# The last layer norm of a two-layer encoder: token tile by token tile, with its scaling done on TensorE

## Chip, cores and metric

One core of one Trainium2 chip runs the whole kernel in one launch. The metric is the device time of that launch in microseconds. Before the change it is 2288.3 us, the median of 3 executions (2286.69 to 2289.38).

## What is computed

A trunk of two layers works on 256 tokens of 2048 features in float32. Each layer is a mixer and a gated MLP, and each of the four sub-layers ends in a residual sum and a layer norm. Cut to what matters here:

```python
def layer_norm(x, g, b):
    mu = jnp.mean(x, axis=-1, keepdims=True)
    var = jnp.mean(jnp.square(x - mu), axis=-1, keepdims=True)
    return (x - mu) * lax.rsqrt(var + LN_EPS) * g + b

for l in range(2):
    ...
    u = x * (1.0 + sc2) + sh2
    y = conv_ffn(u, w_up[l], conv_w[l], conv_b[l], w_down[l])
    x = layer_norm(ALPHA * x + (1.0 + g2) * y, ln_g[l, 1], ln_b[l, 1])
return x
```

The change touches only the last of the four norms, the one whose result is the output.

## The kernel before

The kernel is one hand-ordered program for each engine; semaphores are waited on in the order written. Weights come in units of 2048 columns through four raw slots; ScalarE makes the high part of each (`hi_unit`, L598), VectorE the low part (L939), and TensorE multiplies (L1440 and L1572, L1580) in the one-record format that the profile calls fp32r. The 256 tokens are two token tiles of 128 rows, t = 0 and 1; the 2048 features are four chunks of 512 columns, c or n = 0 to 3. `x` holds both tiles in SBUF.

The end of the program is the phase `(1, "down_b")`: for each chunk c, six units of products into a pair of banks, one bank for each token tile. VectorE's `tail(c)` inside `y_out` (L1040) then multiplies the pair with the gate, adds it to `x`, takes the statistics (`bn_stats`) and, for chunks 0 to 2 of this phase, multiplies `x` with the norm's weight at once (L1076). The very last unit is computed by token tile (`by_tile`, L1444 to L1458): tile 0 is complete (`y_half`) about 2 us before tile 1 (`w_used`), so that VectorE starts on tile 0 (L1045 to L1048) while TensorE works on tile 1 (then L1050 to L1056).

After it comes the last norm, which is in three places:

- TensorE, at the end of its program (L1944 to L1955). It first puts the norm's bias, a product of the identity with `lnp[:, 1]`, into six banks (chunks 0 to 2, two tiles; L1948). Then it waits for `tail_diag` and adds to each of the six banks the product of a diagonal matrix, which holds minus mean times root for every token, with the norm's weight `lnp[:, 0]` (L1953). Both operands of these products are plain f32. "Root" is the reciprocal root of the variance, `rs`.
- VectorE, `layer_norm(3, True)` (L1091 to L1122): the aggregate of the statistics, the variance, the root by ScalarE's Sqrt (L762), a reciprocal and one correction step (L1085 to L1089), the two diagonals (L1104), the whole affine step of chunk 3 in four instructions (L1108, L1112), and then for chunks 0 to 2 one instruction for each bank: `x` times root plus bank (L1119, six instructions).
- SyncE (L577 to L581): four output transfers, one for each chunk with both tiles, 512 KB each, in the order 3, 0, 1, 2, each behind its own count of `ln_affine`.

ScalarE has only the Sqrt in this stretch. Banks: `TAIL_BANKS` gives chunks 0, 1, 2 the banks 0, 4, 6 (plus t); the last chunk's sums are in banks 2 and 3, which the norm doesn't use before.

Of the kernel before, what the change touches and what calls it, by code (L numbers as in the profile page):

```python
# [13 lines left out]
D = 2048  # L14
S = 256
P = 128
F = 5504
KT = D // P
NT = S // P
NCOL = 512  # L20
# [15 lines left out]
EPS = 1e-5  # L36
# [46 lines left out]
OUT_ORDER = [(c, j) for c in (0, 1, 2) for j in (0, 1)] + [(c, j) for c in (0, 1, 2) for j in (2, 3)]  # L83
OUT_ORDER += [(3, j) for j in range(4)]
OUT_BANKS = (0, 2, 4, 0)
TAIL_ORDER = (3, 0, 1, 2)
TAIL_BANKS = {0: 0, 1: 4, 2: 6}
Y_LAST = {((0, "out"), 3): 1, ((0, "down_b"), 3): 2, ((1, "o"), 3): 3, ((1, "down_b"), 3): 4}
OUT_LAST = {IN_UNITS + OUT_ORDER.index((c, 3)): c for c in range(4)}
LR_SLOT, GATE_SLOT = 17, 19  # L90
# [117 lines left out]
def build(nc, A, out):  # L208
# [4 lines left out]
    PH = plan()  # L213

    ctx = ExitStack()
    with ctx:
# [8 lines left out]
        def place(name, shape, at, dt=f32):  # L225
            return nc.alloc_sbuf_tensor_at(name, shape, dt, offset=at)
# [60 lines left out]
        w_lrh = place("w_lr_hi", [P, KT, GRANK], r_s + 10240, f32r)  # L287
        w_lrl = place("w_lr_lo", [P, KT, GRANK], r_s + 10240 + 1024, f32r)
        acc_alt = place("ada_acc_alt", [P, 2 * NCOL], r_s + 4096)
        tail_diag = place("tail_diag", [P, NT, P], r_s)  # L290
        att_hi = place("att_hi", [P, NT, 3 * D], r_w, f32r)

        qkT = place("qk_T", [P, 2, 2 * S], r_s)
# [137 lines left out]
        def _(sp):  # L431
# [142 lines left out]
                    ln_load(2)  # L574
            mlp(1, 16)
            out_v = out[0].rearrange("(t p) n -> p t n", p=P)
            for i, n in enumerate(TAIL_ORDER):  # L577
                sp.wait_ge(sem("ln_affine"), 13 + i)
                sp.dma_start(out_v[:, :, n * NCOL:(n + 1) * NCOL], x[:, :, n * NCOL:(n + 1) * NCOL]
                             ).then_inc(sem("out_done"), 16)  # L580
            sp.wait_ge(sem("out_done"), 4 * 16)  # L581


        @block.scalar
        def _(act):
# [333 lines left out]
                    ins.then_inc(sem("att_p"), 1)  # L919
            ln_sd(2)  # L920
            mlp(1)
            ln_sd(3)


        @block.vector
        def _(dve):
# [109 lines left out]
            def y_out(key, first, stats, banks=(0, 2, 0, 2), ends=None):  # L1036
# [3 lines left out]
                def tail(c):  # L1040
                    y = Y0[key] + c
                    cs = slice(c * NCOL, (c + 1) * NCOL)
                    if (key, c) in Y_LAST:
# [12 lines left out]
                        nc.vector.bn_stats(bn[:, 1, c, :], x[:, 1, cs]).then_inc(y_done, 1)  # L1056
                        return
# [33 lines left out]
            def layer_norm(s, last, after=None):  # L1091
                dve.wait_ge(y_done, {0: 4, 1: 12, 2: 16, 3: 24}[s])
# [4 lines left out]
                if not last:  # L1097
                    ln_quarters(s, 0, 4 if s == 1 else 2)
                dve.wait_ge(sem("ln_var"), s + 1)
                rstd(var, sd, rs, t1, "ln_var", "ln_sd", s + 1)  # L1100
                if last:
                    link(nc.vector.scalar_tensor_tensor(t1, mv[:, :, 0], -1.0, rs, ALU.mult, ALU.mult))
                    for t in range(NT):
                        ins = nc.vector.tensor_scalar(tail_diag[:, t, :], ident, t1[:, t:t + 1], None, ALU.mult)  # L1104
                    ins.then_inc(sem("tail_diag"), 1)
                    cs = slice(3 * NCOL, D)
                    for t in range(NT):
                        ins = nc.vector.scalar_tensor_tensor(x[:, t, cs], x[:, t, cs], mv[:, t, 0:1],  # L1108
                                                             lnp[:, 0, cs], ALU.subtract, ALU.mult)
                    link(ins)  # L1110
                    for t in range(NT):
                        ins = nc.vector.scalar_tensor_tensor(x[:, t, cs], x[:, t, cs], rs[:, t:t + 1],  # L1112
                                                             lnp[:, 1, cs], ALU.mult, ALU.add)
                    ins.then_inc(sem("ln_affine"), 1)
                    for n in range(3):
                        cs = slice(n * NCOL, (n + 1) * NCOL)
                        dve.wait_ge(sem("tail_shift"), n + 1)
                        for t in range(NT):
                            ins = nc.vector.scalar_tensor_tensor(x[:, t, cs], x[:, t, cs], rs[:, t:t + 1],  # L1119
                                                                 bank[TAIL_BANKS[n] + t][:, :], ALU.mult, ALU.add)  # L1120
                        ins.then_inc(sem("ln_affine"), 1)
                    return  # L1122
# [7 lines left out]
                u_lo(U_LN[s], slice(0, 2), 0)  # L1130
                u_lo(U_LN[s] + 1, slice(2, 4), 1)
                lo_unit(after)

            def ln_lo(s, v):
                u_lo(U_LN[s] + v, slice(2 * v, 2 * v + 2), v % 2)
# [149 lines left out]
            for s in range(FRONT_UNITS):  # L1285
# [72 lines left out]
            layer_norm(0, False, unit_no((0, "up_a"), 0, 1))  # L1358
            mlp(0)
            layer_norm(1, False, ATT_U + 1)  # L1360
            o_tail = y_out((1, "o"), True, True, ends={c: ATT_U + s for c, s in O_LAST.items()})
            for u in range(ATT_UNITS):
                if u in SLOT_S:
# [34 lines left out]
                if u < 4:  # L1398
                    ln_affine(1, u)
                beside(ATT_U + u)  # L1400
            layer_norm(2, False, unit_no((1, "up_a"), 0, 1))
            mlp(1)
            layer_norm(3, True)


        @block.gpsimd
# [15 lines left out]
        def _(pe):  # L1422
# [520 lines left out]
            mlp(1)  # L1943
            pe.wait_ge(acc_free, evacuated((1, "down_b"), 2) + 1)  # L1944
            pe.wait_ge(sem("ln_in"), 32 * 4)
            for n in range(3):
                for t in range(NT):
                    nc.tensor.matmul(bank[TAIL_BANKS[n] + t][:, :], ident, lnp[:, 1, n * NCOL:(n + 1) * NCOL],  # L1948
                                     start=True, stop=False)
            pe.wait_ge(sem("tail_diag"), 1)  # L1950
            for n in range(3):
                for t in range(NT):
                    ins = nc.tensor.matmul(bank[TAIL_BANKS[n] + t][:, :], tail_diag[:, t, :],  # L1953
                                           lnp[:, 0, n * NCOL:(n + 1) * NCOL], start=False, stop=True)
                ins.then_inc(sem("tail_shift"), 1)  # L1955


_INS = ["x", "c", "w_ada", "b_ada", "ln_g", "ln_b", "w_in_ab", "w_gate_lr", "b_gate", "gla_norm_g", "w_pool",
# [39 lines left out]
```

## Time and profile before

| | us |
|---|---|
| median of 3 executions | 2288.3 |
| the profiled execution, its own time | 2294.48 |
| span of its trace, first to last instruction | 2292.6 |

| engine | busy us | share of the span |
|---|---|---|
| TensorE, matmuls (PE) | 2241.7 | 98% |
| TensorE, weight loads (PEld) | 1859.4 | 81% |
| VectorE (DVE) | 1695.1 | 74% |
| ScalarE (ACT) | 1009.2 | 44% |
| GpSimd (POOL) | 8.4 | 0% |

The DMA engines move 612.66 MB at a mean of 267 GB/s. The mean granted TensorE clock is 0.990 of full speed. Times in the trace count from the span's start. Matmuls are pipelined and their ends are modelled, so the starts of successive records give the pace, and the sum of their durations doesn't. A plain f32 product of 512 columns shows as two records.

### The profile page before, as it was taken

Reading aid. Unit: us, or ns where it says so; the run is one execution under the profiler, and the core shown is the slowest. Engines: PE = TensorE matmul, PEld = TensorE weight load, DVE = VectorE, ACT = ScalarE, POOL = GpSimd, SP = SyncE. Lnnn points to the kernel's source line nnn. Section 1 sums busy time; section 2 is a strip of 40 time slices with the busy share of each in tenths; the row PEclk is TensorE's granted clock in tenths of the full one; section 3 lists DMA queues with packets and bytes.
Section 4 is the critical chain, followed back from the end, with each engine's and each line's share of the span. In section 5 each row is a group of like instructions: output and inputs, shape, how many; then the busy total and the mean of one; then the engine's idle time right before and its main releaser. Section 6 shows DMA issues by size and latency. Waiting matters only on the chain. (4 is left out here: it accounts for less than half of the span.)

```text
span 2292.6 us, 27917 instructions
## 1 busy us (share of the span) xinstructions
PE 2241.7 (98%) x11205; PEld 1859.4 (81%) x11205; DVE 1695.1 (74%) x1671; ACT 1009.2 (44%) x1011; POOL 8.4 (0%) x19
## 2 busy tenths in 40 slices
PE   7999998999999999999999999999999999999999
PEld 3777776788888888888788888878888888888886
DVE  2889899768888777888877767685688755665665
ACT  2445343454433444443355444435544334445432
POOL 1000000000000000000000000000000000000000
PEclk9999999999999999999999999999999999999999
DMA  9999889867879988789877777865678766566653
GB/s 373 381 409 346 296 298 342 290 201 257 297 269 336 317 274 286 267 281 328 325 262 275 272 262 258 285 240 159 208 259 298 252 200 201 185 192 193 219 191 105
DMA packets 392227, 612.66 MB, mean 267 GB/s; under 512 B 21113, under 2 KB 205073, under 8 KB 390562
## 3 DMA queue, kind: packets, MB, share of 16 engines
q1 hardware_dynamic: 387314, 608.29, 76.0%
q10 hardware_dynamic: 4336, 2.33, 0.3%
q8 instruction: 89, 1.46, 0.2%
q14 instruction: 40, 0.33, 0.0%
q0 software_dynamic: 448, 0.25, 0.0%
HBM read 608.70 MB, written 2.10 MB: 266 GB/s over the span
## 5 line engine op out<-in xcount | busy, mean ns | idle before, releaser
L939 DVE TENSOR_TENSOR w_lo<-w_raw,w_hi 128x2048 fp32r<-128x2048 f32 x380 | 847.8, 2233 | 392.5 <-ACT w_hi L598 342.1
L598 ACT ACTIVATE w_hi<-w_raw 128x2048 fp32r<-128x2048 f32 x380 | 710.1, 1870 | 836.4 <-PE banks L1440 508.2
L1572 PE MATMUL banks<-u_hl,w_hi 128*128 128x512 f32 x2368 | 575.6, 392 | 3.3 <-ACT hid_tok L638 1.8
L1572 PEld LDWEIGHTS banks<-u_hl,w_hi 128*128 128x128 f32 x2368 | 432.9, 188 | 90.3 <-ACT hid_tok L638 2.7
L1440 PE MATMUL banks<-w_hi,u_hl 128*128 128x512 f32 x1920 | 482.1, 404 | 11.4 <-ACT u_hl L663 3.6
L1440 PEld LDWEIGHTS banks<-w_hi,u_hl 128*128 128x128 f32 x1920 | 364.7, 193 | 97.1 <-issue 16.1
L1580 PEld LDWEIGHTS banks<-u_hl,w_lo 128*128 128x128 f32 x2368 | 308.4, 191 | 15.5 <-DVE w_lo L939 1.2
L1580 PE MATMUL banks<-u_hl,w_lo 128*128 128x256 f32 x2368 | 313.3, 283 | 0.3 <-DVE w_lo L939 0.3
L1440 PE MATMUL banks<-w_hi,hid_hi 128*128 128x512 f32 x688 | 270.1, 393 | 0.0
L1440 PE MATMUL banks<-w_hi,hid_lo 128*128 128x512 f32 x688 | 267.8, 389 | 0.0
L955 DVE SCALAR_TENSOR_TENSOR ada_acc<-ada_w,silu_c,ada_acc 128x1024 f32<-128x1024 f32 x187 | 239.3, 1280 | 20.1 <-DMA ada_w<-in_w_ada 14.3
L1440 PE MATMUL banks<-w_lo,u_hl 128*128 128x512 f32 x960 | 238.0, 390 | 2.8 <-DVE w_lo L939 2.8
L1440 PEld LDWEIGHTS banks<-w_lo,u_hl 128*128 128x128 f32 x960 | 180.0, 188 | 41.9 <-DVE w_lo L939 4.5
L1440 PE MATMUL banks<-w_lo,hid_hi 128*128 128x512 f32 x688 | 172.3, 390 | 1.5 <-DVE w_lo L939 1.5
L1440 PEld LDWEIGHTS banks<-w_lo,hid_hi 128*128 128x128 f32 x688 | 128.9, 188 | 29.5 <-DVE w_lo L939 2.8
L1440 PEld LDWEIGHTS banks<-w_hi,hid_hi 128*128 128x128 f32 x688 | 129.2, 188 | 28.7 <-ACT w_hi L598 1.3
L1440 PEld LDWEIGHTS banks<-w_hi,hid_lo 128*128 128x128 f32 x688 | 129.2, 188 | 27.4 <-issue 1.0
L955 DVE SCALAR_TENSOR_TENSOR ada_acc_aux<-ada_w,silu_c,ada_acc_aux 128x1024 f32<-128x1024 f32 x75 | 96.0, 1280 | 7.9 <-DMA ada_w<-in_w_ada 6.2
L837 ACT ACTIVATE conv<-conv 128x512 f32<-128x512 f32 (+1 forms) x44 | 27.4, 623 | 134.6 <-DVE conv L1191 134.6
L955 DVE SCALAR_TENSOR_TENSOR ada_acc_alt<-ada_w,silu_c,ada_acc_alt 128x1024 f32<-128x1024 f32 x48 | 61.6, 1283 | 6.5 <-DMA ada_w<-in_w_ada 3.1
L1191 DVE SCALAR_TENSOR_TENSOR conv<-g_sum,cols,conv 128x255 f32<-128x255 f32 (+1 forms) x148 | 65.0, 479 | 1.4
L623 ACT ACTIVATE g_sum<-banks 128x512 f32<-128x512 f32 (+1 forms) x38 | 22.2, 585 | 95.5 <-PE banks L1580 95.5
(229 smaller groups left out, 1252.1 us busy)
## 6 DMA issues: line engine op xcount, KB each, us to landing
ada_w<-in_w_ada SPq DMA_DIRECT2D x352, 512.0 KB, 6.7
w_raw<-in_w_up SPq DMA_DIRECT2D x344, 512.0 KB, 4.7
w_raw<-in_w_down SPq DMA_DIRECT2D x152, 512.0 KB, 4.9
w_raw<-in_w_qkv SPq DMA_DIRECT2D x96, 512.0 KB, 4.7
w_raw<-in_w_in_ab SPq DMA_DIRECT2D x64, 512.0 KB, 8.9
ada_w_more<-in_w_ada SPq DMA_DIRECT2D x32, 512.0 KB, 11.0
w_raw<-in_w_out_ab SPq DMA_DIRECT2D x32, 512.0 KB, 6.1
w_raw<-in_w_o SPq DMA_DIRECT2D x32, 512.0 KB, 4.9
```

The source lines that it names most:

```text
L598: nc.scalar.activation(whi[:, u % HL_SLOTS, 0:width], raw[:, u % RAW_SLOTS, 0:width], ACT.Copy).then_inc(w_hi, 1)
L623: nc.scalar.activation(g_sum[:, 0:nf, :], pair[b // 2][:, 0:nf, S:2 * S], ACT.Copy).then_inc(g_low, 1)
L837: nc.scalar.activation(gc[:, 0:nf, :], gc[:, 0:nf, :], ACT.Gelu_apprx_tanh).then_inc(h_gelu, 1)
L939: nc.vector.tensor_tensor(wlo[:, u % HL_SLOTS, 0:width], raw[:, u % RAW_SLOTS, 0:width], whi[:, u % HL_SLOTS, 0:width].bitcast(f32), ALU.s ...
L955: nc.vector.scalar_tensor_tensor(acc[:, :], w, silu_c[:, r:r + 1], acc[:, :], ALU.mult, ALU.add).then_inc(a_step, 1)
L1191: ins = nc.vector.scalar_tensor_tensor(gc[:, k, lag:S], src, cols[:, at:at + 1], gc[:, k, lag:S], ALU.mult, ALU.add)
L1440: return nc.tensor.matmul(banks[t][:, 0:width], u_at(kt, t), w[:, slot, k * width:(k + 1) * width], start=start, stop=stop)
L1572: ins = nc.tensor.matmul(bank[banks[s] + i][:, :], tile(whi, k, s, i), uhl[:, kt].rearrange("p a s -> p (a s)"), start=first and k == 0, s ...
L1580: ins = nc.tensor.matmul(bank[banks[s] + i][:, S:2 * S], tile(wlo, k, s, i), uhi[:, kt, :], start=False, stop=last and k == len(kts) - 1)
```

## The change

The last norm is done by token tile. All eight outputs (four chunks, two tiles) now get a bank with bias and mean term on TensorE, chunk 3 in banks 2 and 3. For five of them, all four of tile 0 and chunk 1 of tile 1 (`TAIL_ACT`), TensorE also adds the third term: a second diagonal, of the root itself, times `x` (which has been multiplied with the weight before). The bank then holds the finished output, and ScalarE copies it to `x`. The other three (`TAIL_DVE`: chunks 0, 3 and 2 of tile 1) are finished by VectorE as before. Statistics, root and diagonals are made for each tile by itself, on columns of one element. Each output has its own transfer of 256 KB, eight in all, in the order in which TensorE gets to them. The chain of the correction step is one instruction shorter (r·r·v in one). The early return in `tail` moves the end of chunk 3 into the new function `last_norm`.

```diff
+TAIL_BANKS = {0: 0, 1: 4, 2: 6, 3: 2}
+TAIL_ACT = [(0, 0), (0, 1), (0, 2), (0, 3), (1, 1)]
+TAIL_DVE = [(1, 0), (1, 3), (1, 2)]
...
-        tail_diag = place("tail_diag", [P, NT, P], r_s)
+        tail_diag = place("tail_diag", [P, NT, 2, P], r_s)
...
-            for i, n in enumerate(TAIL_ORDER):
-                sp.wait_ge(sem("ln_affine"), 13 + i)
-                sp.dma_start(out_v[:, :, n * NCOL:(n + 1) * NCOL], x[:, :, n * NCOL:(n + 1) * NCOL]
-                             ).then_inc(sem("out_done"), 16)
-            sp.wait_ge(sem("out_done"), 4 * 16)
+            sent = 0
+            for by, done in ((TAIL_ACT[:4], "tail_act"), (TAIL_DVE[:1], "tail_dve"), (TAIL_ACT[4:], "tail_act"),
+                             (TAIL_DVE[1:], "tail_dve")):
+                for t, n in by:
+                    order = TAIL_ACT if done == "tail_act" else TAIL_DVE
+                    sp.wait_ge(sem(done), order.index((t, n)) + 1)
+                    sp.dma_start(out_v[:, t, n * NCOL:(n + 1) * NCOL], x[:, t, n * NCOL:(n + 1) * NCOL]
+                                 ).then_inc(sem("out_done"), 16)
+                    sent += 16
+            sp.wait_ge(sem("out_done"), sent)
...
-            ln_sd(3)
+            def tail_sd(t):
+                act.wait_ge(sem("tail_var"), t + 1)
+                nc.scalar.activation(sd[:, t:t + 1], var[:, t:t + 1], ACT.Sqrt).then_inc(sem("tail_sd"), 1)
+
+            tail_sd(0)
+            for i, (t, n) in enumerate(TAIL_ACT):
+                if i == 1:
+                    tail_sd(1)
+                act.wait_ge(sem("tail_full"), i + 1)
+                nc.scalar.activation(x[:, t, n * NCOL:(n + 1) * NCOL], bank[TAIL_BANKS[n] + t][:, :], ACT.Copy
+                                     ).then_inc(sem("tail_act"), 1)
...
+            def last_norm():
...
+                def diagonals(t):
+                    v, sdv, r, to = (a[:, t:t + 1] for a in (var, sd, rs, t1))
+                    dve.wait_ge(sem("tail_sd"), t + 1)
+                    link(nc.vector.reciprocal(r, sdv))
+                    link(nc.vector.scalar_tensor_tensor(to, r, r, v, ALU.mult, ALU.mult))
+                    link(nc.vector.tensor_scalar(to, to, -0.5, 1.5, ALU.mult, ALU.add))
+                    link(nc.vector.tensor_tensor(r, r, to, ALU.mult))
+                    nc.vector.tensor_scalar(tail_diag[:, t, 1, :], ident, r, None, ALU.mult)
+                    link(nc.vector.scalar_tensor_tensor(to, mv[:, t, 0:1], -1.0, r, ALU.mult, ALU.mult))
+                    nc.vector.tensor_scalar(tail_diag[:, t, 0, :], ident, to, None, ALU.mult
+                                            ).then_inc(sem("tail_diag"), 1)
+
+                dve.wait_ge(y_done, 23)
+                dve.wait_ge(y_half, 4)
+                link(product(0))
+                link(added(0))
+                variance(0)
+                dve.wait_ge(w_used, unit_no((1, "down_b"), c, PH[1, "down_b"]["n"]))
+                link(product(1))
+                diagonals(0)
+                link(added(1))
+                variance(1)
+                weighted(0).then_inc(sem("tail_g"), 1)
+                diagonals(1)
+                link(weighted(1))
+                for i, (t, n) in enumerate(TAIL_DVE):
+                    cs_n = slice(n * NCOL, (n + 1) * NCOL)
+                    dve.wait_ge(sem("tail_shift"), i + 1)
+                    nc.vector.scalar_tensor_tensor(x[:, t, cs_n], x[:, t, cs_n], rs[:, t:t + 1],
+                                                   bank[TAIL_BANKS[n] + t][:, :], ALU.mult, ALU.add
+                                                   ).then_inc(sem("tail_dve"), 1)
...
+            def tail_base(t, n):
+                nc.tensor.matmul(bank[TAIL_BANKS[n] + t][:, :], ident, lnp[:, 1, n * NCOL:(n + 1) * NCOL],
+                                 start=True, stop=False)
+
+            def tail_from(t, n, of, src, stop):
+                return nc.tensor.matmul(bank[TAIL_BANKS[n] + t][:, :], tail_diag[:, t, of, :],
+                                        src[:, n * NCOL:(n + 1) * NCOL], start=False, stop=stop)
+
+            def tail_whole(t, n):
+                tail_from(t, n, 0, lnp[:, 0, :], False)
+                tail_from(t, n, 1, x[:, t, :], True).then_inc(sem("tail_full"), 1)
+
             for n in range(3):
                 for t in range(NT):
-                    nc.tensor.matmul(bank[TAIL_BANKS[n] + t][:, :], ident, lnp[:, 1, n * NCOL:(n + 1) * NCOL],
-                                     start=True, stop=False)
+                    tail_base(t, n)
             pe.wait_ge(sem("tail_diag"), 1)
+            for t in range(NT):
+                tail_base(t, 3)
             for n in range(3):
-                for t in range(NT):
-                    ins = nc.tensor.matmul(bank[TAIL_BANKS[n] + t][:, :], tail_diag[:, t, :],
-                                           lnp[:, 0, n * NCOL:(n + 1) * NCOL], start=False, stop=True)
-                ins.then_inc(sem("tail_shift"), 1)
+                tail_whole(0, n)
+            pe.wait_ge(sem("tail_g"), 1)
+            tail_whole(0, 3)
+            pe.wait_ge(sem("tail_diag"), 2)
+            tail_from(1, 0, 0, lnp[:, 0, :], True).then_inc(sem("tail_shift"), 1)
+            tail_whole(1, 1)
+            for n in (3, 2):
+                tail_from(1, n, 0, lnp[:, 0, :], True).then_inc(sem("tail_shift"), 1)
```

## Rows read from the trace of the kernel before

**Rows 1.** The chain that ended last, from 2260 us: start, us, what.

```profile
2259.87 17.91 PE banks L1440 x79
2277.78 5.15 PE banks L1948 x12
2282.93 5.16 PE banks L1953 x12
...
2288.11 0.75 DVE x_tok L1119
2288.86 0.66 DVEq L216
```

**Rows 2.** Windows of the end: range, length, busy us of each engine, clock, DMA.

```profile
2277.39:2282.93 5.54, 5.54 (x15) 2.55 (x14) 4.86 (x16) 0.20 (x1) 0.00 (x0) 1.00 0.01 1
2282.93:2288.09 5.16, 5.15 (x12) 1.93 (x11) 5.04 (x8) 0.00 (x0) 0.00 (x0) 1.00 0.35 135
2288.09:2292.60 4.51, 0.00 (x0) 0.00 (x0) 1.41 (x2) 0.00 (x0) 0.00 (x0) 0.97 0.80 310
```

**Rows 3.** Timeline of TensorE's records: start, us, what, count.

```profile
2266.28 1.98 PE L1440 MATMUL banks<-w_lo,hid_hi 128*128 128x512 f32 x8
...
2277.61 5.31 PE L1948 MATMUL banks<-ln_params,consts 128*128 128x512 f32 x12
...
2282.65 0.30 PEld L1953 LDWEIGHTS banks<-ln_params,tail_diag 128*128 128x128 f32 x2 [0.56 <-DVE tail_diag L1104]
2282.76 5.31 PE L1953 MATMUL banks<-ln_params,tail_diag 128*128 128x512 f32 x12
...
2287.48 0.59 PE L1953 MATMUL banks<-ln_params,tail_diag 128*128 128x512 f32 x1
```

**Rows 4.** Timeline of VectorE and ScalarE from the last unit's first half on.

```profile
2275.77 0.69 DVE L1045 TENSOR_TENSOR y_gated<-banks,gate 128x512 f32<-128x512 f32 x1 [5.65 <-PE banks L1440]
...
2276.50 0.69 DVE L1046 SCALAR_TENSOR_TENSOR x_tok<-x_tok,y_gated 128x512 f32<-128x512 f32 x1
...
2277.22 0.69 DVE L1048 BATCH_NORM_STATS2 small<-x_tok 128x6 f32<-128x512 f32 x1
...
2280.00 0.39 DVE L1094 BATCH_NORM_AGGREGATE small<-small 128x2 f32<-128x24 f32 x2
...
2280.42 0.17 DVE L1096 TENSOR_SCALAR small<-small 128x2 f32<-128x2 f32 x1
...
2280.62 0.20 ACT L762 ACTIVATE small<-small 128x2 f32<-128x2 f32 x1 [11.30 <-DVE small L1096]
...
2280.93 0.17 DVE L1085 RECIPROCAL small<-small 128x2 f32<-128x2 f32 x1 [0.34 <-ACT small L762]
...
2281.13 0.16 DVE L1086 TENSOR_TENSOR small<-small 128x2 f32<-128x2 f32 x1
...
2282.12 0.48 DVE L1104 TENSOR_SCALAR tail_diag<-consts,small 128x128 f32<-128x128 f32 x2
...
2285.29 4.23 DVE L1119 SCALAR_TENSOR_TENSOR x_tok<-x_tok,small,banks 128x512 f32<-128x512 f32 x6
...
2288.78 0.74 DVE L1119 SCALAR_TENSOR_TENSOR x_tok<-x_tok,small,banks 128x512 f32<-128x512 f32 x1
```

**Rows 5.** The output transfers, then GB/s in 40 slices from 2289 to 2293.

```profile
L579 SPq DMA_DIRECT2D out_x<-x_tok x4: 372/378/387, 2285.4 to 2289.5; - x4
DMA to landing us min/median/max: 2.7/2.7/2.7
...
GB/s 389 389 471 369 410 389 471 369 410 389 471 369 205 21 164 410 471 369 369 430 471 369 369 430 471 369 369 185 0 0 0 0 0 0 0 0 0 0 0 0
```

**Rows 6.** Issues of the last 112 us by size: count, KB each, median us to landing.

```profile
w_raw<-in_w_down SPq DMA_DIRECT2D x25, 512.0 KB, 4.6
...
w_raw<-in_w_down SPq DMA_DIRECT2D x3, 256.0 KB, 4.2
```

**Rows 7.** ScalarE's groups by line: busy us, mean ns, idle before.

```profile
L889 ACT ACTIVATE qkv<-banks 128x512 f32<-128x512 f32 x24 | 12.8, 585 | 0.0
...
L762 ACT ACT_TABLE_LOAD x3 | 3.8, 1283 | 0.1
```

More of the change, by code:

```diff
@@ L85 @@
 OUT_BANKS = (0, 2, 4, 0)
-TAIL_ORDER = (3, 0, 1, 2)
-TAIL_BANKS = {0: 0, 1: 4, 2: 6}
+TAIL_BANKS = {0: 0, 1: 4, 2: 6, 3: 2}
+TAIL_ACT = [(0, 0), (0, 1), (0, 2), (0, 3), (1, 1)]
+TAIL_DVE = [(1, 0), (1, 3), (1, 2)]
 Y_LAST = {((0, "out"), 3): 1, ((0, "down_b"), 3): 2, ((1, "o"), 3): 3, ((1, "down_b"), 3): 4}
@@ L1042, in tail @@
                     cs = slice(c * NCOL, (c + 1) * NCOL)
+                    if (key, c) == ((1, "down_b"), 3):
+                        return
                     if (key, c) in Y_LAST:
@@ L1089, in rstd, with layer_norm @@
                 link(nc.vector.tensor_tensor(r, r, t, ALU.mult))
-            def layer_norm(s, last, after=None):
-                dve.wait_ge(y_done, {0: 4, 1: 12, 2: 16, 3: 24}[s])
+            def layer_norm(s, after):
+                dve.wait_ge(y_done, {0: 4, 1: 12, 2: 16}[s])
                 for t in range(NT):
@@ L1096, in layer_norm @@
                 nc.vector.tensor_scalar(var, mv[:, :, 1], EPS, None, ALU.add).then_inc(sem("ln_var"), 1)
-                if not last:
-                    ln_quarters(s, 0, 4 if s == 1 else 2)
+                ln_quarters(s, 0, 4 if s == 1 else 2)
                 dve.wait_ge(sem("ln_var"), s + 1)
                 rstd(var, sd, rs, t1, "ln_var", "ln_sd", s + 1)
-                if last:
-                    link(nc.vector.scalar_tensor_tensor(t1, mv[:, :, 0], -1.0, rs, ALU.mult, ALU.mult))
-                    for t in range(NT):
[L1104 to L1122, printed above, removed]
                 half = NCOL // 2
@@ L1132, in layer_norm, with product, added, variance @@
                 lo_unit(after)
+            def last_norm():
+                c = 3
+                cs = slice(c * NCOL, D)
+                b = DOWN_BANKS["down_b"][c]
+                def product(t):
+                    return nc.vector.tensor_tensor(y_tmp[:, t, :], bank[b + t][:, :], gate[:, cs], ALU.mult)
+                def added(t):
+                    return nc.vector.scalar_tensor_tensor(x[:, t, cs], x[:, t, cs], 1.0, y_tmp[:, t, :],
+                                                          ALU.mult, ALU.add)
+                def variance(t):
+                    link(nc.vector.bn_stats(bn[:, t, c, :], x[:, t, cs]))
+                    link(nc.vector.bn_aggr(mv[:, t, :], bn[:, t].rearrange("p c s -> p (c s)")))
+                    nc.vector.tensor_scalar(var[:, t:t + 1], mv[:, t, 1:2], EPS, None, ALU.add
+                                            ).then_inc(sem("tail_var"), 1)
+                def weighted(t):
+                    return nc.vector.tensor_tensor(x[:, t, cs], x[:, t, cs], lnp[:, 0, cs], ALU.mult)
+                def diagonals(t):
[28 more added lines that the diff above has]
+                                                   ).then_inc(sem("tail_dve"), 1)
@@ L1357, in _ @@
                     nc.vector.memset(t1[:, 0:1], 0.0).then_inc(sem("gla_rs"), 1)
-            layer_norm(0, False, unit_no((0, "up_a"), 0, 1))
+            layer_norm(0, unit_no((0, "up_a"), 0, 1))
             mlp(0)
-            layer_norm(1, False, ATT_U + 1)
+            layer_norm(1, ATT_U + 1)
             o_tail = y_out((1, "o"), True, True, ends={c: ATT_U + s for c, s in O_LAST.items()})
@@ L1400, in _ @@
                 beside(ATT_U + u)
-            layer_norm(2, False, unit_no((1, "up_a"), 0, 1))
+            layer_norm(2, unit_no((1, "up_a"), 0, 1))
             mlp(1)
-            layer_norm(3, True)
+            last_norm()
         @block.gpsimd
@@ L1945, in _ @@
             pe.wait_ge(sem("ln_in"), 32 * 4)
+            def tail_base(t, n):
[7 more added lines that the diff above has]
+                tail_from(t, n, 1, x[:, t, :], True).then_inc(sem("tail_full"), 1)
             for n in range(3):
                 for t in range(NT):
-                    nc.tensor.matmul(bank[TAIL_BANKS[n] + t][:, :], ident, lnp[:, 1, n * NCOL:(n + 1) * NCOL],
-                                     start=True, stop=False)
+                    tail_base(t, n)
             pe.wait_ge(sem("tail_diag"), 1)
+            for t in range(NT):
+                tail_base(t, 3)
             for n in range(3):
-                for t in range(NT):
-                    ins = nc.tensor.matmul(bank[TAIL_BANKS[n] + t][:, :], tail_diag[:, t, :],
-                                           lnp[:, 0, n * NCOL:(n + 1) * NCOL], start=False, stop=True)
-                ins.then_inc(sem("tail_shift"), 1)
+                tail_whole(0, n)
[6 more added lines that the diff above has]
+                tail_from(1, n, 0, lnp[:, 0, :], True).then_inc(sem("tail_shift"), 1)
 _INS = ["x", "c", "w_ada", "b_ada", "ln_g", "ln_b", "w_in_ab", "w_gate_lr", "b_gate", "gla_norm_g", "w_pool",
```

## The prediction

> **What bounds the kernel now.** The page of the profile comes first: TensorE has matmuls in flight for 98% of the span. That is an average over a long program, and the change touches only its last 17 us, so the second view is the chain of waits there [rows 1]. The reader is to see one unbroken run of TensorE: 17.91 us of L1440, 5.15 us of the bias products L1948, 5.16 us of the mean products L1953, with no gap between the three, then two VectorE instructions. The third view is the windows [rows 2]: between 2277.39 and 2288.09 TensorE is busy for 5.54 of 5.54 us and 5.15 of 5.16 us, at granted clock 1.00, and VectorE for 4.86 and 5.04 us. Both are nearly full, TensorE quite full. ScalarE works for 0.20 us. The fourth view, the timeline, tells who waits for whom. TensorE's twelve L1948 records begin at 2277.61 and its L1953 records at 2282.76 [rows 3]: 5.15 us for twelve records, which is the same pace across the wait on the diagonal as inside a group. TensorE therefore didn't stand still for the diagonal, though its weight loads did for 0.56 us [rows 3]; the diagonals were ready at 2282.12 + 0.48 = 2282.60 [rows 4], just before TensorE came to them. VectorE's six L1119 instructions follow on each other at 0.66 us, and the fifth starts at 2288.11 [rows 1], 0.04 us behind the modelled end of TensorE's last record at 2287.48 + 0.59 = 2288.07 [rows 3]. By then it had been idle for about 0.1 us (start of the first 2285.29, four at 0.66 us make 2287.93, and the fourth ends a little later). So TensorE sets the end by a hair, VectorE is level with it, and behind both stand the rest of VectorE's last pair (until 2288.78 + 0.74 = 2289.52 [rows 4]) and one transfer of 512 KB, issued at 2289.5 and landed 2.7 us later [rows 5], then 0.4 us to the end of the span at 2292.6.
>
> **What one product costs.** From 2277.61 to 2287.48 there are 23 steps from record to record [rows 3], so one step is 9.87 / 23 = 0.429 us, and a plain f32 product of 512 columns, which shows as two records, takes 0.858 us of TensorE. An fp32r product of the same 512 columns goes at 1.98 us for eight, which is about 0.23 us each [rows 3]. The operands of the norm's products are plain f32 before and after (the diagonals, `lnp` and `x` are all placed as f32), so the dear price applies to each new one.
>
> **TensorE, added.** Before there are 6 bias and 6 mean products: 12. After there are 8 bias products, 8 mean products and 5 root products: 21. The first six bias products are in the same place as before. Nine more products are nine times 0.858 = 7.72 us. Nothing hides them: the stretch they join has no gap on TensorE [rows 2], all 21 stand in one queue, and an output of VectorE's still hangs on the very last of them. The end of TensorE moves from 2288.07 to 2295.79.
>
> That holds only if TensorE waits for nothing on the way, so I place its 21 products at 2277.61 + 0.858 (k - 1) and look at each new wait.
> - Diagonals of tile 0, wanted before product 7 at 2282.76. VectorE does product and sum of tile 0 as before (2275.77 to about 2277.2), statistics to 2277.9, one aggregate (0.39 / 2 = 0.2) and the variance (0.2) to 2278.4, then the product of tile 1 (0.7) to 2279.1 while ScalarE takes the root of tile 0 (0.2, with 0.1 on each side [rows 4]). The small chain steps at 0.2 us (2280.93 to 2281.13 [rows 4]): five of these and two diagonals of 0.24 give 1.5 us, ready at 2280.6. That is 2.1 us early. The aggregate of tile 0 no longer waits for tile 1, which is a true shortening of VectorE's chain by 2.0 us (2282.60 to 2280.6), but nobody collects it: TensorE is still in the bias products.
> - `tail_g`, wanted by product 16: sum of tile 1, statistics, aggregate and variance, weight of tile 0, 2.6 us after 2280.6, so 2283.2. Wanted at 2290.5. Hidden.
> - Diagonals of tile 1, wanted before product 17 at 2291.3. Here ScalarE's order matters: the root of tile 1 is queued behind the first copy, which needs product 10. That ends at 2277.61 + 19 x 0.429 + 0.59 = 2286.35; the copy takes 0.59 (the copy of a 512-column bank, 585 ns [rows 7]), root 0.2, then 1.5 us on VectorE: 2288.8. That is 2.5 us early. VectorE's queue behind this wait holds only the weight of tile 1 and the three outputs, none wanted before 2292. A table load of 1.28 us stands beside Sqrt in three of its four uses [rows 7], behind Gelu or Exp; no copy has one of its own in the trace, and one here would still fit in the 2.5 us.
>
> **VectorE and ScalarE, removed and moved.** Gone from VectorE are four instructions of chunk 3 (L1108, L1112) and three of six L1119, with two weight products and a few small ones added. None of it counts, since TensorE alone now sets the end. What counts is what stands behind TensorE's last product: one L1119-like instruction and not two. Before, VectorE ends 2289.52 - 2288.11 = 1.41 us after its start on the last pair; after, 0.74 us. That saves 0.66 us [rows 1, 4]. The other two VectorE outputs come 0.86 us and more ahead, each 0.74 us long, so they are out of the way. ScalarE's five copies of 0.59 us come at most every 1.7 us; the last, chunk 1 of tile 1, is done near 2294.7. Hidden.
>
> **SyncE and the transfers.** Eight issues and not four, at 0.38 us of SyncE each [rows 5], and TensorE delivers at steps of 0.86 us or more: no queue. The order of the issues is the order of the products. Behind the last VectorE instruction there is now one transfer of 256 KB. The slices of rows 5 split the old one: issued at 2289.5, its bytes run from about 2290.4 to 2291.8 (1.3 to 1.4 us at about 400 GB/s), landed at 2292.2. Half the bytes save 0.65 us: landing in 2.05 us. The transfer ahead of it was issued 0.86 us earlier and is through by then. No row has a small output transfer, so bounds: at the least nothing is saved (landing stays 2.7 us; for loads, 256 KB against 512 KB read 4.2 and 4.6 us [rows 6], only 0.4 us apart), at the most 1.3 us, if the old one's wait in the stream that ran at 389 to 471 GB/s ahead of it [rows 5] goes too. I take 0.65, since rows 5 show the bytes themselves; the row of loads sits near it.
>
> The Trainium skill has a rule that speaks against eight small transfers (DMA: Bandwidth & Descriptors, Anatomy of one DMA and Rules for kernel authors: a fixed cost of about 2 us for each plus bytes at 436 GB/s, so coalesce). Here only the last one's cost is on the path, and the trace disagrees on the size: 2.7 us for 512 KB where the page's fit gives 3.2. By the page, halving the last one saves 0.60 us and the sum would be 0.05 us more.
>
> **The sum,** on the profiled execution: span 2292.6 + 7.72 - 0.66 - 0.65 = 2299.0 us, 6.4 us more; with the 1.9 us around it (2294.48 against 2292.6), 2300.9 us. The median of the runs shown is 2288.3, 6.2 us under the profiled one. The tail's terms are instruction times and should be the same in both, so the forecast is 2288.3 + 6.4 = 2294.7 us, +0.28%. A measurement of this kernel can tell about 0.2% (4.6 us) from no change, so this is slower by a little more than can be told.
>
> **The rivals.**
> - *The last transfer gets no cheaper and the new handovers cost something.* Each side of ScalarE's and TensorE's new semaphores could add some hundredths, and the transfer 0.65 us. For it: no row of a small output. Against: a handover from TensorE to VectorE costs 0.04 us in rows 1 and 3, and only one is on the path. Sum +7.1 to +7.4: 2295.4 to 2295.7 us.
> - *A diagonal comes late.* The wait for tile 1's diagonals would replace nothing and stop TensorE if ScalarE's root were over 2.5 us later than placed. Two table loads (2.6 us) around the first copy would do it by 0.1 us: 2294.8. Cheap even if true.
> - *The change isn't what it says: ScalarE's help relieves an engine that was level with TensorE, and doesn't bind.* This is my forecast's core, not another time; it would be refuted if VectorE had been the bound, and that hangs on the price of TensorE's products. Were TensorE's f32 products at the pace of fp32r ones (0.23 us), nine would cost 2.1 us, against 1.3 us gained behind: +0.8, 2289.1 us, no change. Against it: 23 even steps of 0.429 us.
> - *Not slower: the body runs shorter in the new program.* Everything before 2277.4 is the same work in the same order, but its time isn't fixed: the three executions lie 2.7 us apart, and a changed program may settle elsewhere in that band, since its weight transfers meet the DMA engines at other moments. Price: up to 2.7 us off, 2288.3 + 6.4 - 2.7 = 2292.0 us, +0.16%. It decides from 1.8 us on (6.4 - 4.6). For it: the spread. Against: a median averages most of it, and it goes either way (up to 2297.4 us on the other side). For faster by over 0.2% it would need 11 us, four times the spread.
>
> **How the numbers follow.** Forecast with its bounds (2294.1 to 2295.4): 0.76. Small transfer and handovers: 0.10. Late diagonal: 0.02. Cheap products: 0.02. Shorter body: 0.09. Something unforeseen that gains over 4.6 us: 0.01. Slower by over 0.2% is the first three, 0.88; within 0.2% 0.11; faster 0.01. The range takes the terms' bounds (+5.8 to +7.4) and about 1.5 us of the body's spread on each side: 2292.6 to 2297.2.
>
> **What would show it.** After, the chain of waits should end in some 42 TensorE records of the norm at steps of 0.429 us from 2277.6 to 2295.8 with no gap, one VectorE instruction of 0.74 us, one transfer landing in about 2.05 us. VectorE should stand idle for TensorE before its three outputs, ScalarE before each copy. Tile 0's diagonals should be written near 2280.6 and tile 1's near 2288.8. Wrong would be: a gap in TensorE's records before product 7 or 17 (my placing of VectorE's chain), another pace for products that read `x`, or the same tail with a different time of everything before 2277.4.

## The result, and the profile after

The changed kernel takes 2296.68 us, the median of 6 executions (2293.81 to 2300.9), against 2288.04 us for the kernel before, timed beside it (median of 6, 2285.27 to 2291.32). The ratio is 1.0034, with a 95% interval of 1.0023 to 1.0045: slower by 0.34%, 7.8 us, with 5.3 to 10.3 us in the interval (the two medians by themselves are 8.6 us apart). Its profiled execution took 2296.6 us, with a span of 2294.8 us. That is only 2.2 us above the profiled span of before (2292.6), so the two totals can't be compared as they stand. They can once the trace is cut in two: the *body*, up to the first record of the norm's bias products, and the *tail*, from there to the end of the span.

| | body | tail | span |
|---|---|---|---|
| before | 2277.61 | 14.99 | 2292.6 |
| after | 2273.29 | 21.51 | 2294.8 |

The tail is what the change is about: 6.52 us more. The body does the same work in both and came out 4.3 us shorter in this one execution of after. A span is printed to 0.1 us, so every tail here carries up to 0.05 us of rounding.

The chain that ended last, after (start, us, what); it answers to [rows 1]:

```profile
2249.88 23.57 PE banks L1490 x104
2273.45 6.87 PE banks L1998 x16
2280.32 11.17 PE banks L2002 x26
2291.49 0.03 issue
2291.52 0.75 DVE x_tok L1180
```

The reader is to see again one run of TensorE with no gap, now 6.87 + 11.17 = 18.04 us long in place of 5.15 + 5.16 = 10.31, and one VectorE instruction behind it in place of two. L1998 are 8 bias products, L2002 the 13 others.

The windows of the tail, after (range, length, busy us of PE, PEld, DVE, ACT, POOL, then clock, DMA share, GB/s); they answer to [rows 2]:

```profile
2273.29:2280.16 6.87, 6.87 (x18) 3.04 (x16) 5.04 (x16) 0.20 (x1) 0.00 (x0) 1.00 0.00 1
2280.16:2290.63 10.47, 10.47 (x26) 4.73 (x25) 2.68 (x9) 3.08 (x6) 0.00 (x0) 1.00 0.32 125
```

TensorE is busy in all of both windows, at granted clock 1.00. VectorE, which in [rows 2] was nearly full to the end, now works 2.68 of 10.47 us in the second. The work that it lost has gone to an engine that had no time for it.

The timeline of the three engines, after (start, us, engine, what); it answers to [rows 3, 4]:

```profile
2273.29 7.03 PE L1998 MATMUL banks<-ln_params,consts 128*128 128x512 f32 x16
...
2276.01 0.29 DVE L1161 TENSOR_SCALAR tail_diag<-consts,small 128x128 f32<-128x128 f32 x1
...
2280.16 1.02 PE L2002 MATMUL banks<-ln_params,tail_diag 128*128 128x512 f32 x2
2281.02 1.02 PE L2002 MATMUL banks<-x_tok,tail_diag 128*128 128x512 f32 x2
2281.88 1.02 PE L2002 MATMUL banks<-ln_params,tail_diag 128*128 128x512 f32 x2
...
2282.07 0.60 ACT L938 ACTIVATE x_tok<-banks 128x512 f32<-128x512 f32 x1 [7.68 <-PE banks L2002]
2282.57 0.19 ACT L931 ACTIVATE small<-small 128x1 f32<-128x1 f32 x1
...
2282.80 0.16 DVE L1155 RECIPROCAL small<-small 128x1 f32<-128x1 f32 x1 [4.08 <-ACT small L931]
...
2284.02 0.29 DVE L1161 TENSOR_SCALAR tail_diag<-consts,small 128x128 f32<-128x128 f32 x1
...
2288.16 0.75 DVE L1180 SCALAR_TENSOR_TENSOR x_tok<-x_tok,small,banks 128x512 f32<-128x512 f32 x1 [3.26 <-PE banks L2002]
...
2289.60 1.88 PE L2002 MATMUL banks<-ln_params,tail_diag 128*128 128x512 f32 x4
2290.66 1.60 DVE L1180 SCALAR_TENSOR_TENSOR x_tok<-x_tok,small,banks 128x512 f32<-128x512 f32 x2 [1.75 <-PE banks L2002]
```

Every wait in brackets points at TensorE, except VectorE's 4.08 us for ScalarE's root of tile 1, which cost nothing (below). The product that reads `x` (2281.02) takes the same 0.86 us until the next one starts as the mean product ahead of it. The output transfers, after, against [rows 5]:

```profile
L584 SPq DMA_DIRECT2D out_x<-x_tok x8: 332/333/361, 2282.7 to 2292.3; - x8
DMA to landing us min/median/max: 2.1/2.1/2.2
```

### The profile page after: what moved, and what is told of

Same layout as the page of the kernel before. It is cut to its first block and busy times, and to the rows that moved or that the text cites. A ratio compares the mean times of both kernels' runs of the same rounds, so it can differ in the third digit from the quotient of the medians.

```text
span 2294.8 us, 27967 instructions
## 1 busy us (share of the span) xinstructions
PE 2246.0 (98%) x11223; PEld 1858.6 (81%) x11223; DVE 1693.3 (74%) x1673; ACT 1012.4 (44%) x1017; POOL 8.4 (0%) x19
```

## The experiments

Each line is one kernel: its tail in the profile, and its ratio to the kernel before over several executions, with the 95% interval. The control is the kernel before itself, run as if it were a changed one.

| kernel | tail us | body us of the profiled execution | ratio |
|---|---|---|---|
| before | 14.99 | 2277.61 | |
| control | 15.00 | 2272.20 | 0.9997 [0.9988, 1.0005] |
| after | 21.51 | 2273.29 | 1.0034 [1.0023, 1.0045] |
| after_again | 21.54 | 2276.36 | 1.0033 [1.0020, 1.0046] |
| a_root2 | 21.54 | 2270.16 | 1.0028 [1.0018, 1.0038] |
| b_plus3 | 17.59 | 2273.91 | 1.0016 [1.0006, 1.0026] |
| a_dve8 | 17.22 | 2268.48 | 1.0004 [0.9995, 1.0013] |
| b_fast | 14.82 | 2269.48 | 1.0003 [0.9994, 1.0012] |
| b_split | 14.69 | 2272.01 | 1.0001 [0.9992, 1.0009] |
| a_fast2 | 14.15 | 2277.05 | 1.0004 [0.9996, 1.0013] |
| a_fast | 14.08 | 2271.22 | 0.9997 [0.9988, 1.0006] |
| a_fast3 | 13.44 | 2269.86 | 0.9987 [0.9978, 0.9996] |

Two things stand in the table at once. Tails of the same work repeat within 0.03 us, which is less than the rounding (14.99 and 15.00; 21.51, 21.54 and 21.54). Bodies lie between 2268.48 and 2277.61 us, in no order that goes with the change. A look at the tail alone therefore settles a tenth of a microsecond, and a ratio of totals hardly two.

Where the bodies part can be read from windows. The first 500 us of before, of the control and of a_dve8, which has the shortest body:

```profile
0.00:500.00 500.00, 465.83 (x2180) 358.24 (x2181) 393.47 (x422) 205.86 (x220) 7.40 (x18) 0.97 0.90 327
0.00:500.00 500.00, 467.46 (x2204) 362.62 (x2205) 396.70 (x425) 208.98 (x223) 7.43 (x18) 0.97 0.90 329
0.00:500.00 500.00, 465.53 (x2214) 359.58 (x2215) 398.69 (x425) 209.20 (x223) 7.40 (x18) 0.98 0.91 331
```

At 500 us the kernel before has started 24 records of TensorE fewer than its own control and 34 fewer than a_dve8. From there to 2260 us the counts are 8926, 8926 and 8932. Counted in order, the 2000th record starts at 465.4, 461.0 and 458.8 us: 4.4 and 6.6 us apart from before, where the whole bodies are 5.4 and 9.1 us apart. So most of the difference is made in the first 500 us, far from the change. Its cause isn't shown. The mean granted clock of these three executions goes the same way (0.990, 0.992, 0.994), but a_fast and a_fast2, both at 0.991, have bodies 5.8 us apart.

**The changed kernel again.** 

> The changed kernel once more, unchanged. I split a trace in two: the body, up to the first record of the norm's bias products, and the tail, from there to the end of the span. Before: body 2277.6, tail 15.0 us. After: body 2273.3, tail 21.5 us. Theory (the tail is a chain of fixed durations, the body moves from execution to execution by some us whatever the kernel): tail 21.5 within 0.1 again, a body that differs from 2273.3 by up to some us, and a ratio to the kernel before near 1.0028 (6.5 us). Rival (the new program has a slower body as well, since the first comparison gave 1.0034): a ratio at or above 1.0034 and a body above 2277.

 Measured: tail 21.54, body 2276.36, ratio 1.0033. The tail holds. By the ratio the kernel is 7.5 us slower, beside a tail that explains 6.5, and the interval holds both; the body of 2276.36 is under the rival's 2277. By itself this leaves the rival half open.

**Control.** 

> The kernel before itself, built and timed as one of the changed kernels, against the kernel before. Theory (the tail is fixed and the body moves from execution to execution): tail 15.0 us, a body anywhere from 2268 to 2278 us, ratio 1.0000 with an interval that holds 1; what its ratio is away from 1 is the size that a ratio of these comparisons can have without a cause. Rival (the changed kernels have a body of their own): this one's body lies above all of the changed kernels', of 2268.5 to 2277.1 us so far.

 Measured: tail 15.00, body 2272.20, ratio 0.9997, with an interval from 2.7 us below no change to 1.1 us above it. The rival's condition isn't met: the kernel before has a body of 2272.20 here, in the middle of those of the changed kernels (2268.48 to 2277.05), and had 2277.61 earlier, above them all. Mean time less tail and less the 1.9 us around the span gives the mean body of a kernel, to be compared with the kernel before as timed beside it: 2273.3 against 2271.2 us for the changed kernel (means 2296.68 and 2288.12, six executions each), 2272.2 against 2271.9 for after_again (2295.64 of six, 2288.83 of 28), 2272.5 against 2272.8 for a_root2 (2295.94 of nine, 2289.70 of 32). Single executions of the changed kernel scatter by 2.5 us (standard deviation), so a mean of six is good to 1.0 us, and the differences of +2.1, +0.3 and -0.3 us show no body of its own.

**TensorE's slack.** Diff against the kernel before:

```diff
+            for n, t in ((0, 0), (0, 1), (1, 0)):
+                nc.tensor.matmul(bank[TAIL_BANKS[n] + t][:, :], ident, lnp[:, 1, n * NCOL:(n + 1) * NCOL],
+                                 start=True, stop=True)
             for n in range(3):
                 for t in range(NT):
                     nc.tensor.matmul(bank[TAIL_BANKS[n] + t][:, :], ident, lnp[:, 1, n * NCOL:(n + 1) * NCOL],
```

> The kernel before with three of the bias products done twice ahead of the wait for the diagonals: three more plain f32 products of 512 columns, results unchanged. Theory (TensorE's queue has no slack, each product costs its full 0.858 us): tail 15.0 + 2.57 = 17.6 us, TensorE's records even across the wait. Rival (VectorE's chain sets the end and TensorE only looks full): tail 15.0 to 15.9 us.

 Measured: tail 17.59, 2.60 more than before. VectorE, in b_plus3:

```profile
2278.41 0.48 DVE L1104 TENSOR_SCALAR tail_diag<-consts,small 128x128 f32<-128x128 f32 x2
...
2283.55 1.41 DVE L1119 SCALAR_TENSOR_TENSOR x_tok<-x_tok,small,banks 128x512 f32<-128x512 f32 x2 [1.89 <-PE banks L1956]
2285.27 1.41 DVE L1119 SCALAR_TENSOR_TENSOR x_tok<-x_tok,small,banks 128x512 f32<-128x512 f32 x2 [0.31 <-PE banks L1956]
2286.99 1.41 DVE L1119 SCALAR_TENSOR_TENSOR x_tok<-x_tok,small,banks 128x512 f32<-128x512 f32 x2 [0.31 <-PE banks L1956]
```

The diagonals are ready as early in the tail as before, and now TensorE comes to them later; VectorE waits 1.89 us before its first pair and 0.31 us before each of the other two, where in [rows 4] all six ran in one piece. Each product costs its full price although it stands ahead of a wait. TensorE has no slack.

**VectorE is level.** ScalarE makes rounded copies of weight, bias and identity before the norm, and TensorE multiplies them in fp32r. Diff against the kernel before:

```diff
+        lnp_r = place("ln_params_r", [P, 2, D], r_u, f32r)
+        ident_r = place("ident_r", [P, P], r_u + 2 * D * 4, f32r)
-        tail_diag = place("tail_diag", [P, NT, P], r_s)
+        tail_diag = place("tail_diag", [P, NT, P], r_s, f32r)
...
+            act.wait_ge(w_used, unit_no((1, "down_b"), 0, 1))
+            act.wait_ge(sem("ln_in"), 32 * 4)
+            for k in range(2):
+                nc.scalar.activation(lnp_r[:, k, :], lnp[:, k, :], ACT.Copy)
+            nc.scalar.activation(ident_r[:, :], ident, ACT.Copy).then_inc(sem("tail_r"), 1)
```

> The kernel before with its 12 norm products in fp32r: ScalarE, idle there, makes rounded copies of the norm's weight, bias and the identity ahead of the norm, so the bias and mean terms are rounded. TensorE's 12 products should take 12 x 0.227 = 2.7 us in place of 10.3. Theory (VectorE is level with TensorE, so relief of TensorE alone buys next to nothing): tail 14.8 us, 0.2 less. Rival (TensorE alone binds): up to 3.9 us less, tail near 11 to 12 us.

 Measured: tail 14.82. The end of its chain:

```profile
2273.97 0.48 DVE tail_diag L1111 x2
2274.46 1.33 DVE x_tok L1115 x2
...
2275.82 0.75 DVE x_tok L1119
2276.57 0.66 DVEq L216
2277.23 3.95 DVE x_tok L1126 x6
```

TensorE is gone from it: 7.6 us less work on TensorE bought 0.17 us, since VectorE goes through from diagonals to last output. So the kernel before was balanced to 0.2 us. Relief of TensorE alone was worth no more than that, and load on it costs in full (b_plus3). No run relieves or loads VectorE alone: that the same holds for it is argued from the two levels, not shown.

**Small transfers.** Diff against the kernel before, beside the increments of `ln_affine`, which now come with each instruction:

```diff
-                sp.wait_ge(sem("ln_affine"), 13 + i)
-                sp.dma_start(out_v[:, :, n * NCOL:(n + 1) * NCOL], x[:, :, n * NCOL:(n + 1) * NCOL]
-                             ).then_inc(sem("out_done"), 16)
+                for t in range(NT):
+                    sp.wait_ge(sem("ln_affine"), 13 + 2 * i + t)
+                    sp.dma_start(out_v[:, t, n * NCOL:(n + 1) * NCOL], x[:, t, n * NCOL:(n + 1) * NCOL]
+                                 ).then_inc(sem("out_done"), 16)
```

> The kernel before with eight output transfers of 256 KB in place of four of 512 KB, each behind its own VectorE instruction; nothing else differs. Theory: the last transfer lands in 2.1 us in place of 2.7, tail 14.4 us (0.6 less). Rival (small transfers pay their fixed cost and queue up behind each other, since VectorE delivers 256 KB every 0.66 us and the engines move it in 0.65 us): the last lands in 2.7 us or more, tail 15.0 or above.

 Measured: tail 14.69, 0.30 less: half of what I expected. The transfers of b_split:

```profile
L580 SPq DMA_DIRECT2D out_x<-x_tok x8: 332/332/361, 2279.1 to 2283.9; - x8
...
DMA to landing us min/median/max: 2.1/2.4/2.6
```

In the changed kernel all eight land in 2.1 to 2.2 us, where TensorE delivers an output every 0.86 to 1.72 us and the engines are idle between two. Here one comes every 0.66 us, which is the 0.65 us that its bytes need, and landing rises to a median of 2.4 and up to 2.6. The rival was half right: no transfer lands later than the 2.7 us of the large ones, but of the 0.6 us that I expected only 0.30 is left. That the full stream eats the rest is borne out by a_dve8 (below), where VectorE delivers the same eight transfers every 0.85 us: they land in 2.1 to 2.2 us.

**ScalarE's order.** Diff against the changed kernel:

```diff
             tail_sd(0)
+            tail_sd(1)
             for i, (t, n) in enumerate(TAIL_ACT):
-                if i == 1:
-                    tail_sd(1)
```

> The changed kernel with ScalarE's root of tile 1 ahead of its first copy in place of behind it. Theory (the late diagonal of tile 1 is hidden behind TensorE's queue): tile 1's diagonals are written about 7.0 us after the tail's start in place of 11.0, and the tail stays at 21.5 us. Rival (the wait on the diagonal costs something): tail shorter than 21.3 us.

 Measured: tail 21.54, the same. The last write of tile 1's diagonals begins at

```profile
2276.72 0.29 DVE L1160 TENSOR_SCALAR tail_diag<-consts,small 128x128 f32<-128x128 f32 x1
```

and ends 6.85 us into the tail (2277.01 less 2270.16) in place of 11.02 (2284.31 less 2273.29). Four microseconds on a chain that nobody waits for are worth nothing.

**Without the root products.** `TAIL_ACT` is empty, `TAIL_DVE` holds all eight outputs, TensorE makes only the mean products behind each diagonal (and ScalarE's root of tile 1 is not held by a copy). 

> The changed kernel without the five root products and ScalarE's copies: VectorE finishes all eight outputs, TensorE has 16 products in place of 21, eight transfers as in the change. Theory (TensorE's count of products sets the end): 5 x 0.858 = 4.3 us less than the change, tail 17.2 us, and VectorE waits for TensorE before most of its eight outputs. Rival (ScalarE's help is worth something, VectorE can't keep up with eight): eight instructions of 0.66 us after 7.7 us of the tail would still end at 13.0, ahead of TensorE, so VectorE binds only if the tail comes out above 17.6 us.

 Measured: tail 17.22, 4.29 us less than after: five times 0.858. VectorE keeps up with eight outputs:

```profile
2276.48 6.68 DVE L1179 SCALAR_TENSOR_TENSOR x_tok<-x_tok,small,banks 128x512 f32<-128x512 f32 x8 [0.56 <-PE banks L2001]
```

It waits for TensorE before the first, takes 0.85 us from one to the next, which is TensorE's pace and not its own 0.66, and ends 0.8 us behind TensorE's last record (2283.16 against 2282.37). The root products that ScalarE's help needs cost 4.3 us. The rest of the loss, 2.2 us against before, is chunk 3 on TensorE (four products, 3.43 us) less the shorter end.

**The same order at the low price.** The edit of b_fast, made to the changed kernel; the root products stay f32. 

> The changed kernel with its 8 bias and 8 mean products in fp32r from rounded copies that ScalarE makes ahead of the norm (bias and mean terms are rounded); the five root products stay plain f32. TensorE's work falls from 21 x 0.858 = 18.0 us to 16 x 0.227 + 5 x 0.858 = 7.9 us. Theory (the new order by token tile is good, only the price of f32 products ruins it): the next bound is VectorE's chain for tile 1, diagonals at 7.0 us, last output at 10.0, tail 12.4 us, that is 2.6 less than the kernel before and 9.1 less than the change. Rival (waits of the new order or the transfers bind next): tail 14 us or more.

 Measured: tail 14.08, 0.91 less than before and 7.4 less than after, where I expected 2.6 and 9.1. Its chain names the larger part of what I left out:

```profile
2273.94 0.30 DVE tail_diag L1170
2274.24 0.04 issue
2274.29 0.73 PE banks L2008 x2
2275.02 5.91 PE banks L2013 x17
2280.93 0.03 issue
2280.96 0.75 DVE x_tok L1189
```

and VectorE's outputs of tile 1 show what it cost:

```profile
2279.72 0.75 DVE L1189 SCALAR_TENSOR_TENSOR x_tok<-x_tok,small,banks 128x512 f32<-128x512 f32 x1 [0.74 <-PE banks L2013]
2280.96 1.41 DVE L1189 SCALAR_TENSOR_TENSOR x_tok<-x_tok,small,banks 128x512 f32<-128x512 f32 x2 [0.49 <-PE banks L2013]
```

TensorE is still in it. The two bias products of chunk 3 stand behind the wait on the first diagonal, though they don't need it, and TensorE then needs about 1.09 us for each of tile 0's four outputs, so it comes to tile 1 about 8 us into the tail. VectorE had written tile 1's diagonals at 7.2 us; its first output starts at 8.5. The two waits are 1.2 of the 1.7 us by which the tail is longer than expected; the rest is the end, 2.9 us from VectorE's last output to the end of the span where I had 2.4. I had counted each output's time and neither the queue in front of tile 1 nor a fuller stream of transfers. a_fast2 changed only what comes behind that, ScalarE's root first and the order of tile 1's last outputs. 

> As the changed kernel with bias and mean products in fp32r, and in addition ScalarE's root of tile 1 ahead of its first copy, and the mean products of tile 1's chunks 3 and 2 ahead of the root product of its chunk 1, whose output goes out last. Theory: VectorE's three outputs run without a gap from 7.7 us on, tail 12.2 us, 0.2 less than without the new order. Rival: the two ends are set by the same chain and nothing changes, 12.4 us.

 Measured: tail 14.15, the same as a_fast to the rounding. The rival is right that nothing changes, though at 14.1 and not at its 12.4 us: tile 1's diagonals are ready at 6.8 us, and VectorE's first output still starts at 8.5.

**The queue in the right order.** Diff against a_fast, TensorE's part (ScalarE's list loses its fifth output to VectorE, and the transfers follow the new order):

```diff
-            pe.wait_ge(sem("tail_diag"), 1)
+            pe.wait_ge(acc_free, evacuated((1, "down_b"), 3) + 1)
             for t in range(NT):
                 tail_base(t, 3)
+            pe.wait_ge(sem("tail_diag"), 1)
             for n in range(3):
                 tail_whole(0, n)
-            pe.wait_ge(sem("tail_g"), 1)
-            tail_whole(0, 3)
             pe.wait_ge(sem("tail_diag"), 2)
-            tail_from(1, 0, 0, lnp_r[:, 0, :], True).then_inc(sem("tail_shift"), 1)
-            tail_whole(1, 1)
-            for n in (3, 2):
+            for n in (0, 3, 2, 1):
                 tail_from(1, n, 0, lnp_r[:, 0, :], True).then_inc(sem("tail_shift"), 1)
+            pe.wait_ge(sem("tail_g"), 1)
+            tail_whole(0, 3)
```

> The changed kernel with bias and mean products in fp32r (bias and mean terms are rounded), and in addition chunk 3's bias products ahead of the wait for the diagonals, ScalarE's root of tile 1 first, the four mean products of tile 1 ahead of the last root product of tile 0, and only four root products: VectorE finishes all of tile 1. Theory (without it, TensorE's queue of bias products behind the wait and of root products ahead of tile 1 held VectorE until 8.5 us): VectorE's four outputs start at 7.5 us and end at 10.2, the last transfer, in a full stream, lands in 2.4 to 2.6 us, tail 13.0 to 13.2 us. Rival (the transfers' stream sets the end): 14.1 us as without it.

 Measured: tail 13.44 us, ratio 0.9987 [0.9978, 0.9996]: the shortest tail of all, 1.55 us under before and 0.64 under a_fast. The ratio alone would be weak evidence: it says 3 us, twice what the tail gives, and its interval overlaps the control's. VectorE's four outputs and the transfers:

```profile
2277.37 2.72 DVE L1189 SCALAR_TENSOR_TENSOR x_tok<-x_tok,small,banks 128x512 f32<-128x512 f32 x4
...
DMA to landing us min/median/max: 2.1/2.2/2.6
GB/s 451 389 410 267 369 410 471 369 389 389 390 369 389 389 369 492 328 328 410 410 410 389 430 410 389 410 410 430 389 348 62 0 0 0 0 0 0 0 0 0
```

VectorE runs from 7.51 to 10.23 us of the tail without a gap, as expected. From there to the end it takes 3.21 us (after: 2.54). The last row is the moved GB/s in 40 slices from 2279.3 to 2283.3: full for 3 us up to the last byte. I had expected 2.8 to 3.0 us from VectorE's end on (a tail of 13.0 to 13.2 less 10.2), so the miss of 0.2 to 0.4 us lies in this full stream. Whether VectorE or the stream would bind a further change wasn't tested.

## Why the prediction was right

I forecast 6.4 us more on the tail, 2294.7 us with a range of 2292.6 to 2297.2, and slower by over 0.2% at 0.88. The tail took 6.52 us more, the measured median is 2296.68 us, and the whole interval of the ratio lies above 0.2%, if only just (1.0023; after_again has 1.0020 and a_root2 1.0018 at its lower end). So the mechanism and the tail's size are right. The total is less well hit: 2296.68 us lies above the band of 2294.1 to 2295.4 that had most of the chance, and 0.5 us inside the range. That it stayed inside is in part luck. By its steps:

- *Price of a product.* 0.858 us. After, the first of TensorE's 42 records starts at 2273.29 and the last four run to 2289.60 + 1.88 = 2291.48; the end moved from 10.46 to 18.19 us into the tail, 7.73 us for nine products. b_plus3 (2.60 for three) and a_dve8 (4.29 for five) give it two more times.
- *No slack on TensorE.* Right, by the unbroken chain and by b_plus3.
- *VectorE level, not the bound.* Right, by b_fast (0.17 us).
- *Diagonals.* Tile 0 placed 3.0 us into the tail (2280.6), found written at 3.01 (2276.30); tile 1 placed at 11.2 (2288.8), found at 11.02. Hidden, by a_root2. The copies on ScalarE took 0.60 us each and no table load stands between them and the roots, so the rival of the late diagonal falls.
- *One VectorE instruction behind the end.* 0.66 us placed. It ends 18.97 us into the tail in place of 11.91, 7.06 later, so 0.67 saved.
- *The last transfer.* Placed at 2.05 us, found at 2.1 to 2.2; from VectorE's end to the end of the span 2.54 us in place of 3.08, so 0.54 saved, where I took 0.65. The rival (no gain) falls for this kernel, whose outputs are far apart; in b_split, with an output every 0.66 us, half of it comes true. The fit that the prediction takes from the Trainium skill (DMA: Bandwidth & Descriptors, Anatomy of one DMA) is stated there for transfers issued from GpSimd, and these are issued from SyncE: 256 KB landed in 2.1 us where the fit gives, as an estimate, 2.6, and 512 KB in 2.7 where it gives 3.2.
- *Sum of the tail:* 7.73 - 0.67 - 0.54 = 6.52 us.
- *The body.* I left its spread at the 2.7 us of three executions. It is wider: 2268.5 to 2277.6 in twelve profiles, and before ran from 2285.45 to 2292.55 us in one set of 28, and from 2285.48 to 2296.54 in another of 32. With a median of 6 executions against such a spread, the 1.3 to 2.1 us by which the total passed the tail's 6.5 (by the ratio and by the medians) are of the size that chance gives. The term that was mis-sized is this one: 1.5 us on each side was too little, and the range held because the tail's terms were close.

That the total lay above the forecast isn't explained by anything in the tail. The mean bodies above agree within their scatter; that the changed program has a body slower by a fraction of a microsecond isn't excluded. In the profiles compared above most of a body's difference is made in the first 500 us; why stays open.

## What to carry to other kernels

Before moving work to an idle engine, count what must be added on the engine that feeds it: ScalarE was idle and had room for its copies of 0.60 us, but each brought TensorE a product of 0.86 us on a queue without a gap. Where two engines are level to 0.2 us, relief of one gains next to nothing: b_fast made TensorE's products cheap and gained 0.17 us. With the work shared and done by token tile as well, a_fast gained 0.91 us, and with the queue in the order of need and ScalarE's fifth output given to VectorE, a_fast3 gained 1.55. How much of it the sharing, the order by tile and the smaller transfers gave, each by itself, wasn't taken apart. Where totals scatter by several microseconds, cut the trace at an event that both kernels share and compare the part that changed.

## What the runs showed of the hardware that I had not expected

- A transfer of 256 KB to the output lands in 2.1 us when the engines are idle between two (after: 2.1 to 2.2 for all eight), and in up to 2.6 us when another is issued every 0.66 us (b_split), hardly less than one of 512 KB (2.7, [rows 5]). A spacing of 0.85 us is enough for 2.1 to 2.2 us (a_dve8).
- Executions of one and the same kernel differ by up to 11 us (before, 2285.48 to 2296.54 us in 32 executions), while a tail of 15 or 21.5 us repeats within 0.03 us. Between before and its control, 4.4 of 5.4 us are lost in the first 500 us.
- A mean product in fp32r, with a plain f32 root product behind it in the same bank, keeps its low price: the pair takes 1.09 us from one output to the next (a_fast), which is 0.23 and 0.86.
